# Turning five of eight blocks of h by VectorE and ScalarE where TensorE turned them, in a hybrid transformer block of one core

## What is computed

```python
mod = cond @ w_ada[l] + b_ada[l]
u = _modulate(_rmsnorm(h, norm1_g[l]), sh1, sc1)
h = h + 0.5 * gt1 * _swiglu(u, ffn1_w_in[l], ffn1_w_out[l])
u = _modulate(_rmsnorm(h, norm2_g[l]), sh2, sc2)
h = h + gt2 * _hybrid_mixer(u, ..., w_out[l])
u = _modulate(_rmsnorm(h, norm3_g[l]), sh3, sc3)
h = h + 0.5 * gt3 * _swiglu(u, ffn2_w_in[l], ffn2_w_out[l])
return _rmsnorm(h, final_g)
```

## Time and profile before

| what | us |
|---|---|
| median of 3 runs | 2107.68 |
| lowest and highest | 2106.69, 2109.64 |
| the profiled execution, its own time | 2106.88 |
| its span, first to last instruction | 2105.1 |
| work before and behind the span (2106.88 - 2105.1) | 1.8 |

### The profile page before, as it was taken

One profiled execution on the slowest core, in us unless ns is written; L12 is line 12 of the kernel. 1 busy time (PEld: TensorE's weight loads), 2 busy tenths in 40 slices (PEclk: granted clock), 3 DMA queues, 4 the chain that ended last, 5 costly groups with the idle time before them and its releaser, 6 DMA issues.

```text
span 2105.1 us, 24025 instructions
## 1 busy us (share of the span) xinstructions
PE 2076.3 (99%) x9483; PEld 1718.7 (82%) x9483; DVE 1579.8 (75%) x1879; ACT 997.2 (47%) x1253; POOL 4.6 (0%) x22
## 2 busy tenths in 40 slices
PE   7999999999999999999999999999999999999998
PEld 6788888888888878888888888888888888888887
DVE  6987987888788888787555789778875466755666
ACT  4577433443334455446555654554443444434444
POOL 0000000000000000000000000000000000000000
PEclk9999999999999999999999999999999999999999
DMA  9998998997899778975555679658665565555554
GB/s 357 387 385 300 335 319 321 327 338 279 300 332 338 280 248 295 323 271 162 160 160 160 218 276 339 245 207 285 228 219 190 190 199 192 188 200 192 189 179 160
DMA packets 249600, 540.79 MB, mean 257 GB/s; under 512 B 11920, under 2 KB 14352, under 8 KB 248720
## 3 DMA queue, kind: packets, MB, share of 16 engines
q1 hardware_dynamic: 249104, 539.12, 73.6%
q10 hardware_dynamic: 384, 0.13, 0.0%
HBM read 537.10 MB, written 2.11 MB: 256 GB/s over the span
## 4 chain that ended last, share of the span: by engine, by line
PE 92%; DVE 3%; DMA 1%; ACT 1%; issue 1%; SPq 1%; ACTq 0%; DVEq 0%
PE pa L678 15%; PE pa L681 15%; PE pa L680 15%; PE pb L678 15%; PE pb L681 14%; PE pb L680 14%; DVE ada_acc L1594 1%; PE px L693 1%; DMA raw<-in_ffn_w_in_dram 1%; ACT hi L1127 1%; DVE proj L2152 0%; DMA ada_s<-in_w_ada_dram 0%; DVE lo L1574 0%; PE px L753 0%; PE pm L1007 0%
## 5 line engine op out<-in xcount | busy, mean ns | idle before, releaser
L1127 ACT CAST hi<-raw 128x1024 fp32r<-128x1024 f32 (+1 forms) x732 | 750.7, 1030 | 981.0 <-PE pa L681 476.0
L1574 DVE TENSOR_TENSOR lo<-raw,hi 128x1024 fp32r<-128x1024 f32 (+1 forms) x732 | 868.8, 1197 | 443.4 <-ACT hi L1127 442.2
L678 PE MATMUL pa<-hi,act_hi 128*128 128x512 f32 (+1 forms) x1056 | 414.3, 392 | 7.6 <-DVE act_lo L1641 4.4
L681 PE MATMUL pa<-hi,act_lo 128*128 128x512 f32 (+1 forms) x1056 | 408.7, 387 | 0.0
L680 PE MATMUL pa<-lo,act_hi 128*128 128x512 f32 (+1 forms) x1056 | 408.4, 387 | 0.0
L678 PE MATMUL pb<-hi,act_hi 128*128 128x512 f32 x1024 | 402.4, 393 | 0.0
L681 PE MATMUL pb<-hi,act_lo 128*128 128x512 f32 x1024 | 398.7, 389 | 0.0
L680 PE MATMUL pb<-lo,act_hi 128*128 128x512 f32 x1024 | 398.5, 389 | 0.0
L1672 DVE SCALAR_TENSOR_TENSOR ada_acc<-ada_w,cond,ada_acc 128x1024 f32<-128x1024 f32 (+1 forms) x240 | 275.4, 1148 | 6.2
L678 PEld LDWEIGHTS pa<-hi,act_hi 128*128 128x128 f32 x1056 | 198.8, 188 | 51.2 <-DVE act_lo L1641 5.4
L681 PEld LDWEIGHTS pa<-hi,act_lo 128*128 128x128 f32 x1056 | 198.6, 188 | 41.1
(11 more groups left out here) (317 smaller groups left out, 1432.5 us busy)
## 6 DMA issues: line engine op xcount, KB each, us to landing
raw<-in_ffn_w_in_dram SPq DMA_DIRECT2D x176, 1024.0 KB, 5.1
ada_w<-in_w_ada_dram SPq DMA_DIRECT2D x224, 512.0 KB, 6.1
raw<-in_ffn_w_out_dram SPq DMA_DIRECT2D x64, 1024.0 KB, 5.1
raw<-in_w_in_dram SPq DMA_DIRECT2D x64, 1024.0 KB, 5.1
ada_s<-in_w_ada_dram SPq DMA_DIRECT2D x64, 512.0 KB, 10.6
raw<-in_ffn_w_out_dram SPq DMA_DIRECT2D x32, 768.0 KB, 4.5
raw<-in_w_out_dram SPq DMA_DIRECT2D x16, 1024.0 KB, 6.3
raw<-in_w_att_up_dram SPq DMA_DIRECT2D x8, 1024.0 KB, 5.1
```

The costliest lines, as they stand in the source:

```text
L678: pe.matmul(ps, a_hi[:, k0 + kk, tok], w_hi, start=start and kk == 0, stop=False, skip_group_check=on)
L681: mm = pe.matmul(ps, a_lo[:, k0 + kk, tok], w_hi, start=False, stop=stop and kk == n - 1, skip_group_check=on)
L1127: act.copy(hi_of(ph, i, j, half)[:, 0:n, 0:w], raw[:, j % RING, 2 * half:2 * half + n, 0:w])\
L1574: dve.tensor_tensor(lo[:, j % RING, s, 0:w], raw[:, j % RING, s, 0:w], hi_of(ph, i, j, half)[:, 0:n, 0:w].bitcast(F32), ALU.subtract)\
```

## The change

For n = 1 two blocks (0 and 1) and for n = 2 three blocks (0, 1 and 2) are no longer turned by PE. For each of them DVE, right behind add_out of unit 3, transposes all 32x32 squares of the block in place order from h into buf_a, in one instruction of 128x1024. ACT then copies the squares to their partitions of n_t with 16 copies of 32 partitions by 256 elements: 4 behind unit 5, 6 behind unit 6, 6 behind unit 7; four activations in place scale n_t by the gain behind unit 7. DVE gets a wait for these copies (ht_mv) before it writes buf_a again, in the next add_out and in last_gated of tile 0. The evacuations of the PE blocks stay for the others; for n = 2 those of groups 4 and 5 leave norm(). The DMAs and SP's order are not touched.

```diff
--- before.py
+++ after.py
@@ -187,6 +187,10 @@
 
     BY_DVE = [plan[name].nat0 + i for name, n in (("ffn2_in0", PARTS[0]), ("ffn2_in1", PARTS[1]),
                                                   ("ffn2_in2", PARTS[2] - 1)) for i in range(n)]
+
+    H_BY_ACT = {1: 2, 2: 3}
+    H_ON_PE = {n: 8 - 2 * b for n, b in H_BY_ACT.items()}
+    H_PE0 = {1: 0, 2: H_ON_PE[1]}
 
     OUT_AT = {0: (0, 1), 1: (2,), 2: (3,), 3: (4,), 4: (5,), 5: (6,), 6: (7,)}
 
@@ -340,6 +344,8 @@
         cols_done = sem("cols_done")
         pv_ok = sem("pv_ok")
         ht_mm = sem("ht_mm")
+        ht_sq = sem("ht_sq")
+        ht_mv = sem("ht_mv")
         ht_ok = sem("ht_ok")
         nt_t = sem("nt_t")
         nt_hi = sem("nt_hi")
@@ -746,7 +752,7 @@
 
             def h_turn(n, g):
 
-                if g >= 2:
+                if g >= 10 - H_ON_PE[n]:
                     pe.wait_ge(ht_ok, 8 * (n - 1) + g - 1)
                 for k in (0, 1):
                     for tt in range(TT):
@@ -825,7 +831,7 @@
                         if b == 0 and k0 <= 4 * (kn - 1) < k0 + n:
 
                             pe.wait_ge(nat_lo, 2 * (nat_last + 1))
-                        if norm and norm < 3 and b > 0 and (j, half) == (2, 0):
+                        if norm and norm < 3 and b > H_BY_ACT[norm] and (j, half) == (2, 0):
                             pe.wait_ge(h_ok, H_BLOCKS[norm] + b)
                             h_turn(norm, 2 * b - 2)
                             h_turn(norm, 2 * b - 1)
@@ -1160,12 +1166,32 @@
 
             def h_evac(n, g):
 
-                act.wait_ge(ht_mm, 8 * (n - 1) + g + 1)
+                act.wait_ge(ht_mm, H_PE0[n] + g - (8 - H_ON_PE[n]) + 1)
                 act.wait_ge(gain_ok, 8 + n)
                 for k in (0, 1):
                     ins = act.activation(n_t[:, 2 * g + k, :], px[:, g % 2, k * T:(k + 1) * T], ACT.Identity,
                                          scale=gain[:, 2 * g + k:2 * g + k + 1])
                 ins.then_inc(ht_ok, 1)
+
+            def h_blocks(n, b, blocks):
+
+                act.wait_ge(ht_sq, H_BY_ACT[1] * (n - 1) + b + 1)
+                for m in blocks:
+                    tb, fb = m // 4, m % 4
+                    src = buf_a[32 * tb:32 * (tb + 1), :, :].rearrange("p t (f b q) -> p t f b q", f=4, b=4)[:, :, :, fb, :]
+                    dst = n_t[32 * fb:32 * (fb + 1), 4 * b:4 * b + 4, :]\
+                        .rearrange("p f (t b q) -> p t f b q", t=TT, b=4)[:, :, :, tb, :]
+                    ins = act.copy(dst, src)
+                if blocks[-1] == 15:
+                    ins.then_inc(ht_mv, 1)
+
+            def h_gain(n, b):
+
+                act.wait_ge(gain_ok, 8 + n)
+                act.wait_ge(ht_mv, H_BY_ACT[1] * (n - 1) + b + 1)
+                for k in range(4 * b, 4 * b + 4):
+                    ins = act.activation(n_t[:, k, :], n_t[:, k, :], ACT.Identity, scale=gain[:, k:k + 1])
+                ins.then_inc(ht_ok, 2)
 
             def out_phase(ph, kn, nat_last, sq=None, norm=0):
                 for b in range(4):
@@ -1177,9 +1203,10 @@
                             squares(sq + b, b - 1)
                         if b == 3 and n_ == 3 and norm:
                             root_table()
-                        if 0 < b < 3 and n_ == 7 and norm:
-                            h_evac(norm, 2 * b - 2)
-                            h_evac(norm, 2 * b - 1)
+                        if norm and 0 < b <= H_BY_ACT[norm] and n_ in (5, 6, 7):
+                            h_blocks(norm, b - 1, {5: range(0, 4), 6: range(4, 10), 7: range(10, 16)}[n_])
+                        if norm and 0 < b <= H_BY_ACT[norm] and n_ == 7:
+                            h_gain(norm, b - 1)
 
             def turn_affine(g, count, scale, bias):
                 act.wait_ge(xt_mm, count + 1)
@@ -1249,8 +1276,9 @@
                 if n_ == 2:
                     half_root(n, 0)
                 if n_ == 3:
-                    h_evac(n, 4)
-                    h_evac(n, 5)
+                    if H_BY_ACT[n] < 3:
+                        h_evac(n, 4)
+                        h_evac(n, 5)
                     norm_hi(n, sh, 1)
                     norm_hi(n, sh, 2)
                     half_root(n, 1)
@@ -1871,6 +1899,8 @@
 
             def last_gated(n, ph, gate, tt):
 
+                if tt == 0 and n < 3:
+                    dve.wait_ge(ht_mv, H_BY_ACT[1] * (n - 1) + H_BY_ACT[n])
                 if tt == 0:
                     dve.wait_ge(tt_done, n)
                 else:
@@ -2005,7 +2035,14 @@
                             if name == "ffn1_out0" and b == 3:
                                 gate_row((2,))
                             if b > 0:
+                                n = {"ffn1_out2": 1, "wout": 2}.get(name)
+                                if n and 1 < b <= H_BY_ACT[n] + 1:
+
+                                    dve.wait_ge(ht_mv, H_BY_ACT[1] * (n - 1) + b - 1)
                                 add_out(ph, b - 1, gate)
+                                if n and b <= H_BY_ACT[n]:
+                                    dve.wait_ge(h_ok, H_BLOCKS[n] + b)
+                                    dve.transpose(buf_a[:, :, :], h[:, :, (b - 1) * NC:b * NC]).then_inc(ht_sq, 1)
                         if name == "ffn2_out2" and b > 0 and n_ == 6:
                             times_final(b - 1, None)
                         if (b, n_) == (1, 1) and name == "ffn1_out2":
```

## The result

| | before | changed |
|---|---|---|
| median, us | 2108.14 (5 runs) | 2119.46 (5 runs) |
| lowest and highest | 2106.69, 2109.64 | 2118.48, 2120.04 |
| ratio, 95% interval | | 1.0052 [1.0041, 1.0064] |
| span of the profiled execution | 2105.1 | 2117.7 |

A forecast was written before the change was run, and what follows sets the result against it. PE, busy 2076.3 of 2105.1 us, was taken to bound the kernel. Norm 1 at 0 and norm 2 at +1.05 were taken as +0.9, giving 2107.8, or 2108.6 as median; 8 in 10 range 2104.6 to 2112.4.

The forecast's parts named there:

- What PE saves: ffn1_out2 and wout: 0.89 us a block no longer turned by PE, 4.45 us for five blocks, the most possible.
- What DVE gets: One 128x1024 transposition a block behind add_out of unit 3, taken as 1.3 us, ahead of unit 4's lo.
- What ACT gets: 16 copies a block at 0.31 us each, 4.9 us, plus activations and a wait: 6.65 us a block.
- no surcharge: DVE's 32x256 and 128x1024 rows, read as 1.05 ns a column and 166 fixed, nothing extra for strides or 32 partitions.
- the ledger: Account by pass of savings and stalls in both norms: norm 1 0, norm 2 +1.05, taken as +0.9 in all.
- ACT is again just in time: End of ffn1_out2's pass 2: lo for pass 3 ready at 764.6 for a need of 764.8.
- the tail: Wout's pass 3 and the norm: ACT ends late, so PE waits 3.0 us instead of 0.65 before ffn2_in0.
- Norm 1 comes to 0: ffn1_out2: saving of 1.8 us offset by stalls of 0.2 and 1.35, with rounding a net of 0.
- norm 2 to +1.05: wout and its norm: all the saving is lost in the wait before ffn2_in0, and 1.05 us with it.
- Rival 2: ACT's copies take over 0.31 us: slower by over 0.2% from 0.38 on, 2126 at 0.61; chance 0.12.
- Rivals 1, 3 and 4: 1: saving arrives, 2103.2 (0.04, smaller gain 0.24); 3: late weights, 2110 (0.05); 4: 272 ns a transposition, 2096.8 (0.01).

The follow-up runs named there:

- DVE's part alone: The change with no ACT copies; the scaling activations read the squares unmoved, so the placing is left out: 2106.35 us, 0.9990 of the kernel before.
- norm1_only: The change for norm 1's two blocks only, wout as in the kernel before: 2113.81 us against 2108.67, ratio 1.0025.
- twelve_copies: The change with 12 ACT copies a block instead of 16, part of h turned to wrong places: 2109.81 us against 2108.67 for the kernel before.
- fill: The whole change plus 16 unread PE transpositions at the start of passes 2 and 3 of ffn1_out2: 2117.27 us against 2108.01 for the kernel before.

## Why the prediction was wrong, step by step

- **What PE saves**, 0.89 a block: right. In the kernel without copies a pass of ffn1_out2 takes 16.32 us, 0.90 under the 17.22 of before. But no saving of PE was left anywhere in the whole change.
- **What DVE gets**: right in the main. 1.25 us x 5, and DVE shows no wait for the copies. Its stall in wout's pass 1 was put at 1.65 and is 1.52, and 1.31 in DVE's part alone. The one in ffn1_out2's pass 2, put at 1.35, is 1.01 to 1.05 in norm1_only, twelve_copies and fill, and absent in the changed kernel, where the half clock stands in its place.
- **What ACT gets** is the step that failed: "two of them began at 978.80 and the next instruction at 979.41, so 0.31 each". The length of a copy was right, the distance wasn't: 0.415. 16 copies cost 6.6 us and not 4.9. The row taken was a pair in the same partitions; the new copies change them each time. DVE's row for this very shape, 32x256, was read for its length only and not for how its neighbours follow, which the row at 1426.80 above would have shown. And "no surcharge" could not be read from it: 1.05 ns a column and 166 fixed are two numbers worked out from two rows. The 1.7 us fell where the ledger had written "ACT is again just in time": the stall before pass 2 was put at 0.1 to 0.2 and is 2.06, the one before pass 3 at 0 and is 2.06 (1.70 where the clock stayed up). Wout's pass 2 was put at 0 and is 1.29: ACT's delay made DVE late. In the tail PE was to wait 3.0 at the first unit of ffn2_in0; it stood 3.21 us, earlier, at the spreading of the row (L767).
- **Norm 1 comes to 0, norm 2 to +1.05**: by one norm at a time they are +5.1 and +3.9. With ACT's load as predicted the sum is +1.1 for a forecast of +0.9, and its stretches are +0.3 and +1.0, so the rest of the ledger held, to within the interval of -0.4 to +3.6. Term by term it is less exact: the stalls at unit 4 are 1.0 and 1.1 for 1.35 and 1.65, and the wait at norm 2 is 1.4 and 1.0 for 3.0.
- **The clock** stood nowhere in the prediction. Waits were priced at their length. The profile of the kernel before has a wait of 1.99 at the norm with the full clock behind it, so nothing in it showed the risk. Fill gives 2 us for two of the four falls; the third, in proj, isn't the change's.
- **Rival 2**, slow copies, is the one that came, for another reason than strides. It was to decide from 0.38 a copy on; at 0.415 its rule gives 16 x 0.105 x 3 = 5.0 and +0.9, so 2113.6. Of the other 5.8 us the profile gives 1.3 to wout's pass 2, and the falls of the clock account for most of the rest, though no run prices them all; the rival had neither. The sign that the prediction named for it, copies over 0.5, didn't show: their mean is the expected 0.40, since the loss is in the distance and not in the length. Its chance of 0.12 was too low for a shape of which no row existed on that engine.
- Rivals 1, 3 and 4 didn't come: nothing of the saving is left, DVE's part alone shows no late weights, and a block is worth 0.9 us and not 2.2 (8 x 0.272).

## What to carry to other kernels

A chain of small instructions is priced by the distance between their starts, not by the length of one: look for a row in which the same shape follows itself with the same change of partitions. Where the busiest engine runs at 99%, ask of every engine that feeds it how late it may be at each unit; 3% more work for ACT, crowded into a few units, cost 13.6 us: the change is 11.3 slower than the kernel before, and DVE's part alone was 2.3 faster. And a saving of 0.2% on the bounding engine isn't worth a wait of 2 us on it, since the clock may fall behind that wait.

## What the runs showed of the hardware

- ACT copies of 256 columns begin 0.31 us apart when source and target start in the same group of 32 partitions as in the copy before, and 0.41 when either changes; 64 partitions in turn are the same, and the strides of the runs don't matter. Eight DVE copies of this shape take 1.70 us with a fixed pair and 2.37 with another group each time.
- Behind waits of PE of 1.99 to 3.2 us the granted clock was at half (1.2 GHz) for some 3.4 us in some executions, and stayed full in others behind 1.99 and 2.05. With 16 transpositions in the place of two waits of 2.06 it stayed full in the profile, and the kernel was 2 us faster.
